# A token combination and its low part moved from VectorE to GpSimd, in the first steps of two feed-forward stages

## What is computed

```python
def swiglu(h, w_in, w_out):
    gu = h @ w_in
    gate, up = jnp.split(gu, 2, axis=-1)
    return (jax.nn.silu(gate) * up) @ w_out

        h = rmsnorm(x, norm_ffn[i]) * (1 + sc2) + sh2
        x = x + g2 * swiglu(h, ffn_w_in[i], ffn_w_out[i])
```

## Time and profile before

| | us |
|---|---|
| median of 3 runs | 2804.91 |
| lowest and highest of them | 2804.58, 2808.41 |
| the profiled execution | 2804.34 |
| its span, first to last instruction | 2802.3 |
| busy time of PE, DVE, ACT, POOL in it | 2684.2, 1951.9, 1020.1, 271.6 |
| mean granted clock of PE | 0.977 of full |
| largest item of the chain that ended last | PE, 38% of the span |

### The profile page before, as it was taken

One profiled execution on the slowest core, in us unless ns is written; L12 is line 12 of the kernel. 1 busy time (PEld: TensorE's weight loads), 2 busy tenths in 40 slices (PEclk: granted clock), 3 DMA queues, 4 the chain that ended last, 5 costly groups with the idle time before them and its releaser, 6 DMA issues. The chain is left out here.

```text
span 2802.3 us, 35494 instructions
## 1 busy us (share of the span) xinstructions
PE 2684.2 (96%) x12770; PEld 2111.9 (75%) x12770; DVE 1951.9 (70%) x3283; ACT 1020.1 (36%) x1797; POOL 271.6 (10%) x422
## 2 busy tenths in 40 slices
PE   6999699999999999999998989999999999999998
PEld 5666377788888888766775777888888877878867
DVE  6787747877777777767766598777777785432635
ACT  5554424333333333354444253333333341101233
POOL 2110000000000000101100000000000029930000
PEclk9999899999999999999999899999999999979999
DMA  5222421111111111212321111111111131112122
GB/s 226 97 99 95 147 89 50 50 54 51 54 55 49 56 53 46 101 62 92 97 91 76 31 35 57 53 52 53 55 50 55 54 102 43 48 39 47 38 83 76
DMA packets 170923, 193.09 MB, mean 69 GB/s; under 512 B 7968, under 2 KB 136192, under 8 KB 170400
## 3 DMA queue, kind: packets, MB, share of 16 engines
q1 hardware_dynamic: 158256, 147.45, 16.3%
q0 software_dynamic: 12560, 44.20, 5.2%
HBM read 177.86 MB, written 12.58 MB: 68 GB/s over the span
## 5 line engine op out<-in xcount | busy, mean ns | idle before, releaser
L2145 DVE SCALAR_TENSOR_TENSOR xT<-psum,mod,xT 128x1024 f32<-128x1024 f32 x352 | 446.2, 1279 | 144.0 <-PE psum L1278 144.0
L1278 PE MATMUL psum<-hT_high,w_low 128*128 128x512 f32 x1344 | 360.0, 390 | 4.1 <-DVE xT L2145 4.0
L1278 PEld LDWEIGHTS psum<-hT_high,w_low 128*128 128x128 f32 x1344 | 251.8, 188 | 58.6 <-DVE xT L2145 6.6
L1663 ACT ACTIVATE w_high<-wpair 128x512 fp32r<-128x512 f32 x294 | 184.6, 632 | 227.6 <-DMA wpair<-in_ffn_w_in_dram 129.9
L1059 PE MATMUL psum<-hT_high,w_low 128*128 128x512 f32 x880 | 243.4, 395 | 3.0 <-DVE arena L2541 2.1
L1278 PE MATMUL psum<-h_low,w_low 128*128 128x512 f32 x672 | 207.6, 390 | 2.2 <-DVE h_low L2140 2.2
L1106 PE MATMUL psum<-hT_high,w_low 128*128 128x512 f32 x480 | 203.7, 424 | 2.4 <-DVE h_low_mix L2429 1.7
L1246 PE MATMUL psum<-hT_high,w_high 128*128 128x512 f32 x504 | 196.8, 391 | 3.3 <-DVE w_low L2105 3.3
L1782 ACT ACTIVATE arena<-arena 128x384 f32<-128x384 f32 (+3 forms) x320 | 157.6, 494 | 116.3 <-DVE arena L2326 116.3
L1059 PEld LDWEIGHTS psum<-hT_high,w_low 128*128 128x128 f32 x880 | 167.4, 191 | 39.3 <-DVE arena L2541 2.3
L1247 PE MATMUL psum<-h_low,w_high 128*128 128x512 f32 x504 | 196.6, 390 | 0.0
(11 more groups left out here) (345 smaller groups left out, 5259.8 us busy)
## 6 DMA issues: line engine op xcount, KB each, us to landing
wpair<-in_ffn_w_in_dram SPq DMA_DIRECT2D x176, 256.0 KB, 2.9
wpair<-in_ffn_w_out_dram SPq DMA_DIRECT2D x88, 256.0 KB, 2.8
wpair<-in_ada_tiles_dram POOLq DMA_DIRECT2D x20, 1024.0 KB, 5.3
wpair<-in_ada_tiles_dram POOLq DMA_DIRECT2D x32, 512.0 KB, 3.6
wpair<-in_w_in_dram SPq DMA_DIRECT2D x24, 512.0 KB, 3.7
wpair<-in_b_tiles_dram SPq DMA_DIRECT2D x18, 512.0 KB, 3.3
arena<-in_ada_tiles_dram SPq DMA_DIRECT2D x8, 1024.0 KB, 16.3
out_dram<-xT SPq DMA_DIRECT2D x16, 512.0 KB, 3.0
```

Source lines behind the costliest of these rows:

```text
L1278: mm = nc.tensor.matmul(dst[:, HALF * t:HALF * t + HALF], w, src[:, t, :], start=n == 0, stop=n == 2)
L1663: nc.scalar.activation(part_high[name], part_raw[name], ACT.Copy).then_inc(part_high_ready, 1)
L2145: nc.vector.scalar_tensor_tensor(xT[:, m, :], acc[m % 2] if src is None else src, mod[:, l, 40 + m:41 + m], xT[:, m, :], ALU.mult, ALU.add ...
```

## The change

In the first steps of both feed-forward stages GpSimd makes T4 = T4 - T2, in two halves of channels (128x1024 each), and T4's low part (128x2048); VectorE no longer does. GpSimd's first half waits for the first half of T2, the second for the second half, the low part for T4's high part, which ScalarE makes once both halves are there. Two new semaphores count this. VectorE's T2 low part has a new wait, for both halves of T4. `token_made` and `token_split` now count one less in each stage. P4 of step 1 waits for GpSimd's low part.

```diff
@@ (GpSimd's list)
+            def last_token(f):
+
+                for n in range(2):
+                    pool.wait_ge(token_made, 7 * f + n + 6)
+                    v = token_raw["T4"][:, 2 * n:2 * n + 2]
+                    nc.gpsimd.tensor_tensor(v, v, token_raw["T2"][:, 2 * n:2 * n + 2], ALU.subtract).then_inc(last_token_made, 1)
+                pool.wait_ge(token_high_ready, 4 * f + 4)
+                nc.gpsimd.tensor_tensor(token_low["T4"], token_raw["T4"], as_f32(token_high["T4"]), ALU.subtract).then_inc(last_token_split, 1)
+
+            last_token(0)
             pool.wait_ge(product_done, product_number(0, STEPS - 1, "P4"))
...
+            last_token(1)
             pool.wait_ge(product_done, product_number(1, STEPS - 1, "P4"))
@@ (TensorE, step)
                     if first:
-                        pe.wait_ge(token_split, 4 * f + 4)
+                        pe.wait_ge(last_token_split, f + 1)
                     with_token(s, "P4", "A22", "e", "T4", False)
@@ (ScalarE, token)
-                    act.wait_ge(token_made, 8 * f + n + 4)
+                    if name == "T4":
+                        act.wait_ge(last_token_made, 2 * f + 2)
+                    else:
+                        act.wait_ge(token_made, 7 * f + n + 4)
@@ (VectorE, token_lows)
                     dve.wait_ge(token_high_ready, 4 * f + n + 1)
+                    if name == "T2":
+                        dve.wait_ge(last_token_made, 2 * f + 2)
@@ (VectorE, second_step)
                     add_down(0, 1)
-                    token(3, "T4", "T4", "T2", slice(0, 4))
                     token_lows(2, "T2")
                     low(1, "S1")
                     add_down(0, 2)
                     token_lows(0, "T1")
                     low(1, "A22")
                     add_down(0, 3)
-                    token_lows(3, "T4")
                     combine(2, "S3")
```

More of the change, by code:

```diff
@@ L497, in two_blocks_kernel @@
         token_split = sem("token_split")
+        last_token_made = sem("last_token_made")
+        last_token_split = sem("last_token_split")
         ssm_landed = sem("ssm_landed")
@@ L1290, in step @@
                     if first:
-                        pe.wait_ge(token_split, 4 * f + 1)
+                        pe.wait_ge(token_split, 3 * f + 1)
                     else:
@@ L1299, in step @@
                     if first:
-                        pe.wait_ge(token_split, 4 * f + 2)
+                        pe.wait_ge(token_split, 3 * f + 2)
                     with_token(s, "P6", "S2", "a", "T2", False)
@@ L1304, in step @@
                     if first:
-                        pe.wait_ge(token_split, 4 * f + 3)
+                        pe.wait_ge(token_split, 3 * f + 3)
                     with_token(s, "P5", "S1", "a", "T1", False)
@@ L2074, in low @@
                     if n in (1, 3) and k < 4:
-                        dve.wait_ge(token_made, 8 * (n // 2) + k + 1)
+                        dve.wait_ge(token_made, 7 * (n // 2) + k + 1)
                     at = 24 * (n % 2) + k
@@ L2122, in token @@
                 def token(n, name, x, y, ks):
-                    dve.wait_ge(token_made, 8 * f + n + 4)
+                    dve.wait_ge(token_made, 7 * f + n + 4)
                     nc.vector.tensor_tensor(token_raw[name][:, ks], token_raw[x][:, ks], token_raw[y][:, ks], ALU.subtract).then_inc(token_made, 1)
```

## The result

| us | before | after |
|---|---|---|
| median of 8 runs | 2805.64 | 2813.65 |
| lowest, highest | 2803.83, 2808.41 | 2811.57, 2816.87 |
| the profiled execution | 2804.34 | 2813.81 |
| its span | 2802.3 | 2811.9 |

The ratio is 1.0026, with a 95% interval of 1.0017 to 1.0036: the change makes the kernel slower, by 8.0 us between the medians.

The account below looks back on a forecast made before the run. PE bounds the kernel, but waits for VectorE in each feed-forward stage's first steps. Lateness of 2.7 us at P5, 5.4 for two stages, plus 1.6 for a clock fall, sums to 7.0 on 2804.34: 2811.3 us, range 2803.5 to 2815.5.

Parts of the forecast that it names:

- the clock: First steps of both stages: PE's granted clock halves behind idle time; three falls for two, +1.6 us.
- Step 1: First stage: GpSimd's first half of T4 blocks combine S2 until 486.1; A12's low part and P2 0.55 us late.
- Step 2: First stage: GpSimd's second half of T4 blocks S4's low part, ending at 495.96 for 494.22, 1.74 us late.
- Step 3: First stage: VectorE skips its 2.20 us, T2's low part ends at 501.76, P6 starts 0.46 us earlier.
- Steps 4 and 5: First stage: T4's high part ends at 502.4; GpSimd's low part then blocks T1's low part; P5 2.7 us late.
- The rule weighed there: Beside GpSimd's SBUF reads: two-SBUF-input VectorE instructions are kept out for its whole instruction, 4.51 us for the low part.
- (b): At T1's low part: shorter block, GpSimd's low part gives way or comes later; 2805.1, up to 2808; chance 0.07.
- Step 6: From P4 on: P4 finds its parts ready, all that follows is 2.7 us late; +5.4 us for two stages.
- (a): First steps: engines don't hold each other up, P6 2.20 us earlier in both stages; 2799.9 or 2798.3; chance 0.08.
- (c): GpSimd's subtractions slower, low part 5.2 us, P5 3.9 us late; 2815.3 with two extra clock falls; chance 0.08.
- (d): GpSimd's subtractions cheaper, 4.2 and 2.1 us, P5 1.9 us late; 2808.1 without an extra clock fall; chance 0.15.

Follow-up runs that it names:

- the combination alone: Changed kernel with only T4 = T4 - T2 on GpSimd in its two halves, T4's low part back on VectorE: 2804.94 us, ratio 0.9996 to before.
- placed quarters: Changed kernel with three 128x512 combination parts on GpSimd beside PSUM-reading instructions, the fourth and T4's low part on VectorE: 2801.29 us, 0.9982 to before.
- low behind A22: Changed kernel with GpSimd's low part of T4 also waiting for A22's low part: 2806.08 us, ratio 0.9997 to before.
- low part only: Changed kernel with only T4's low part on GpSimd, the combination back on VectorE: 2812.34 us, ratio 1.0023 to before.
- one-input low: Changed kernel with T4's low part replaced by a one-input GpSimd multiplication by zero over 128x2048: 2803.12 us, one run.
- the kernel with fills: Changed kernel with all three GpSimd subtractions replaced by zero fills, T4 left out: 2798.09 us, ratio 0.9969 to before.

## Why the prediction was right, point by point

**Direction and size.** 2811.3 forecast, 2813.65 measured, within 2803.5 to 2815.5; slower by over 0.2%, which had 0.55. The mechanism was the forecast one, and its share of the time was sized too small: 5.4 us for two stages where the positions at P5 give 3.5 + 3.2 = 6.7. Against the medians 8.0 us, that leaves 1.3 for the clock and the rest, for which I had 1.6. Of the 2.3 us between 2811.3 and 2813.65, 1.3 is therefore P5; another 1.3 is the base, since I added to one execution of 2804.34 and the median of eight is 2805.64; the clock and the rest take 0.3 off.

**Step 1.** combine S2 was to last 1.8: it took 1.82 in the second stage. A12's low part was to be 0.55 late and was 1.06 and 0.98 late (4.00 and 3.92 behind the first gate product for 2.94). This is the term that was mis-sized. I let S4 start 0.08 ahead of S2's end and A12's low part likewise, as instructions in a list do; but S4 waits for S2, and started about 0.1 behind it, and the low part another 0.10 behind S4. In the kernel before, the gap ahead of S4 lay under a wait of 0.26 us for a load; the one ahead of A12's low part could be read there, 0.10 as well (485.26 + 0.69 to 486.06). The rest is GpSimd's start, 0.17 and 0.08 behind the first gate product where I had 0.08, and its 2.40 for 2.35.

```profile
485.26 0.69 DVE L2120 TENSOR_TENSOR wpair<-wpair 128x512 f32<-128x512 f32 x1 [0.26 <-DMA wpair<-in_ffn_w_in_dram]
```

**Step 2.** S4's low part was to last 1.9: 1.94 in the second stage, and 1.43 in the first, where add_down(0, 0) ahead of it had to wait for PE, whose clock had fallen, so that S4's low part began later and ended where it would have. It ended 2.32 and 2.24 late for 1.74, carrying step 1's error.

**Step 3.** P6 was to be 0.46 earlier; it was 0.12 later and 0.03 earlier. The 2.20 us removed and the 2.2 us of blocking cancel. The run with the combination alone shows the same by itself.

**Steps 4 and 5.** T4's high part started 18.1 and 17.8 behind the gate product for 17.35, GpSimd's low part 20.1 and 19.8 for 19.3, and took 4.59 for 4.51. T1's low part took 5.88 and 5.66 for 5.6 and ended 2.15 after GpSimd's, to the digit. P5: 3.5 and 3.2 late for 2.7. The error of 0.5 from step 1 runs through to here, and 0.1 is GpSimd's price. The 0.3 by which the first stage is later than the second begins with GpSimd's first half, 0.09 later there; the rest comes from a clock fall (see below).

**The rule weighed there.** The rule of the Trainium skill (SBUF — State Buffer, "Who interferes with whom") holds at the size that mattered: 4.59 us of GpSimd kept a two-input instruction out to its end, fills did not, instructions with an input in PSUM passed. It did not hold to the end for GpSimd's one-input instruction, which kept VectorE out for 3.63 of its 5.37 us. Rival (b)'s giving way about each microsecond did not occur for a subtraction.

**Step 6.** PE's late waits are 1.53 and 1.13 as before (1.51 and 1.12), and all between is shifted. One thing I did not name: in step 2 of the first stage PE waits another 1.85 us, for a down product's weights that landed late. ScalarE's row after, then the one of before:

```profile
533.42 0.63 ACT L1661 ACTIVATE w_low<-wpair 128x512 fp32r<-128x512 f32 x1 [4.57 <-DMA wpair<-in_ffn_w_out_dram]
```

```profile
529.40 0.63 ACT L1648 ACTIVATE w_low<-wpair 128x512 fp32r<-128x512 f32 x1 [2.73 <-DMA wpair<-in_ffn_w_out_dram]
```

The load was issued at 528.07 after the change and took 5.3 us to be read, 3.5 before (issued at 525.88). Such waits in step 2, of 0.2 to 1.9 us, also occur in some stages of kernels with no late P5 (placed quarters 1.16, low behind A22 1.33), so they aren't shown to be the change's. They go with the clock: of the 24 stages profiled, twelve have a clock fall right behind the two late waits of step 2, the first stage before among them, and none of these has the further wait; the seven further waits all lie in the other twelve. At full clock PE is sooner at the down product whose weights are still on their way (7.6 us behind the 1.13 us wait after, 9.0 behind the 1.12 us wait before), so part of what a spared fall gives back goes into this wait.

**The clock.** Three falls for two were forecast. PE's windows of 1 us in the profile after have four:

```profile
487.00:488.00 1.00, 1.00 (x4) 0.50 0.00 0
507.00:508.00 1.00, 0.84 (x2) 0.50 0.00 0
538.00:539.00 1.00, 1.00 (x4) 0.50 0.00 0
1678.00:1679.00 1.00, 1.00 (x4) 0.50 0.27 77
```

The first lies ahead of P6, where PE had to wait for VectorE anyway (0.39 instead of 1.48 us), and cost P6 nothing. It did cost P5 about 0.2 us: P3 was done later, ScalarE's copy of it (L1702) waited for it and started 17.61 behind the first gate product for 17.32, and T4's high part and GpSimd's low part stand behind that copy.

```profile
497.84 0.60 ACT L1702 ACTIVATE hT<-psum 128x512 f32<-128x512 f32 x1
```

The others follow the P5 wait in each stage and the 1.85 us wait in step 2. Over three kernels with a long P5 wait (changed, low part only, one-input low) the six stages have nine falls; over the other nine, before among them, eighteen stages have fourteen. The extra falls fit the idle time, but a profile each is too little to price them.

**Rivals.** (a), no blocking, is excluded by every run with a subtraction; its time, 2799.9 or 2798.3, is what the kernel with fills shows, 2798.09. (b) is excluded by T1's low part, 5.88 and 5.66 us instead of plain. (c) and (d) differed from the forecast by GpSimd's price, which came out 0.08 above my value.

## What to carry to other kernels

Work that is moved from VectorE to GpSimd isn't gone from VectorE: while a GpSimd subtraction ran here, of 1.3 to 4.6 us, the next VectorE instruction with two SBUF inputs stood still to its end, so a move pays only where it runs beside instructions with an input in PSUM, or where VectorE has nothing due. Cut GpSimd's work into instructions no longer than those gaps, and give each a wait that starts it there; here three placed quarters of the combination, with the fourth quarter and the low part back on VectorE, gave 0.18% faster in place of 0.26% slower. In a sum over a list that is delayed, count the gaps of dependent instructions too: a wait that covered them is no cover once they move.

## What the runs showed of the hardware that I had not expected

A GpSimd instruction whose recorded start lay 0.18 us before the end of VectorE's current one did not go next, in either stage: VectorE's following instruction did. I had taken the one that waits first to be served first; at such distances, by recorded starts, that does not hold. Whether GpSimd begins to read only some time behind its recorded start is not shown.

A one-input GpSimd instruction of 5.37 us held VectorE's two-input one back, but let it in after 3.63 us, while a subtraction of 4.59 us held it to its end. And GpSimd's multiplication of one input by a number was slower than its subtraction of two: 5.37 for 4.59 us over 128x2048, though its end ran beside VectorE's instruction, so that its plain length isn't shown. In the kernel before, the same multiplication over 128x384 (L842) took 1.17 us at its shortest, the subtraction (L826) 1.00.
